# State-space impulse responses with full-width stationary operands, and a batch's outputs turned directly ahead of the next batch's readout

## The chip, the cores and the metric

One NeuronCore of one Trainium2 chip runs the whole program. Its engines work side by side, each through its own instructions strictly in order: TensorE (PE in the rows; its weight loads, PEld, are a track of their own and may run beside a matmul), VectorE (DVE), ScalarE (ACT), GpSimd (POOL) and SyncE (SP). The last two mostly issue transfers here. Engines wait for each other through semaphores that only count up. The metric is the device time of one launch in microseconds. The kernel before has a median of 3036.04 us over 3 runs (3035.94 to 3036.09).

## The reference

The program is one layer of a state-space and pooling block followed by an attention and feed-forward block, 512 tokens wide 2048, all in fp32. What matters here is the state-space mixer, 64 groups of 16 channels with 64 complex states:

```python
bu_re = jnp.einsum('blgc,gnc->blgn', u32, bb_re)
bu_im = jnp.einsum('blgc,gnc->blgn', u32, bb_im)
...
_, _, s_re, s_im = lax.associative_scan(
    _scan_combine, (a_re_t, a_im_t, bu_re, bu_im), axis=1)
y = (jnp.einsum('blgn,gcn->blgc', s_re, c_re.astype(f32))
     - jnp.einsum('blgn,gcn->blgc', s_im, c_im.astype(f32))
     + d_skip.astype(f32).reshape(N_SSM_GROUPS, SSM_GROUP) * u32)
```

The mixer's input is a quarter of `rmsnorm(x) @ w_in`, a product of 512 x 2048 with 2048 x 4096.

## The kernel before, in words

The input product is cut into 32 units n = 0 to 31 of 128 output columns. A unit is 16 tiles with three matmuls each (`products`, lines L1539 to L1541): the weights are split into a high and a low part (WH by ScalarE, WL by VectorE), the activations too (XH, XL), and high x high, high x low and low x high are added up in a PSUM bank. Between two units TensorE's program has small blocks of the state-space mixer. The 64 groups are treated in eight batches t of eight groups, and the 512 tokens in 64 chunks of 8 (CQ = 8, NCH = 64). For a batch:

- VectorE forms H, the output rows times powers of the transition (`impulse`), and BF, the input rows (`drive_rows`). TensorE multiplies them in `kernels` (L1673): for each group g the 16 columns of BF are the stationary operand, 128 columns of H move, and 16 rows come out in banks 2 and 3. ScalarE copies these rows to KS (`kernel_copies`, which counts ks_ready), and SyncE lays them out eight times as the banded matrix TZ (`kernel_rows`).
- VectorE forms G, TensorE turns it (`drives_turned`, L1684, banks 4 and 5), ScalarE copies it to GT.
- `chunk_states` (L1696): GT x U, the states that each chunk adds, in bank 6. ScalarE copies them to SL; SyncE swaps the two halves of the partitions into SSW (`states_swapped`); VectorE runs the scan over chunks (`scan`, L2306), which gives RR.
- SyncE swaps RR into RSW (`scan_swapped`); VectorE forms SV, the state carried into each chunk (`carried`, L2316 and L2319, counts sv_ready).
- `readout` (L1714), bank 7: first 8 matmuls U x TZ (within a chunk), then 8 matmuls SV x H (carried in). Each has a stationary operand of 64 columns, and they alternate between the upper and the lower 64 output rows.
- ScalarE copies bank 7 to YS (`token_copy`, counts ys_ready). `tokens_turned` (L1724) turns YS into bank 2 by 16 matmuls of 64 x 64 with the identity, again in alternating halves, and counts yt_done. VectorE adds the result to the input times d_skip (`y_out`, L2324, counts y_read).

Nothing schedules this at run time; the order is written out by the unit number n. On TensorE, behind unit 8 + 3t stand `chunk_states(t)` and `kernels(t + 1)`, behind unit 9 + 3t `readout(t)`, behind unit 10 + 3t `drives_turned(t + 1)` and `tokens_turned(t)`; batch 7 is shifted by one unit. The other engines have loops over the same n. A plain fp32 matmul is one instruction in the program and two records in the trace (a transpose is one record), so that `kernels` has 8 matmuls and 16 records for a batch.

The YS buffer lies at the same place as RSW (60 K). SyncE's copy into RSW has these waits, which the diff does not touch:

```python
def scan_swapped(t):

    sp.wait_ge(r_ready, t + 1)
    if t >= 1:
        sp.wait_ge(yt_done, t)
    sp.dma_start(RSW[0:64, :], RR[64:128, :]).then_inc(r_swapped, 16)
    sp.dma_start(RSW[64:128, :], RR[0:64, :]).then_inc(r_swapped, 16)
```

In SyncE's loop it stands in turn n = 9 + 3t, behind `states_swapped(t)` and the load of RAW for unit n + 3 (for t = 7 in turn 29).

Of the kernel before, what the change touches and what calls it, by code (L numbers as in the profile page):

```python
# [25 lines left out]
P = 128  # L26
S = 512
# [5 lines left out]
SSM_GROUPS, SSM_C, SSM_N = 64, 16, 64  # L33
MIX_TILES = 8
# [94 lines left out]
CQ = 8  # L129
# [42 lines left out]
def build(nc, w_units, w_ada, c_row, x_t, p_t, vec_d, con_d, mask_d, ssm_par, ssm_bc, w_pool_d,  # L172
# [3 lines left out]
    def at(name, off, shape, dt=FP32):  # L176
        return nc.alloc_sbuf_tensor_at(name, shape, dt, offset=base + off)

    K = 1024
# [41 lines left out]
    IDENT = CON[:, C_ID:C_ID + P]  # L221
# [18 lines left out]
    SSW = at("SSW", 56 * K, [P, S])  # L240
    RR = at("RR", 58 * K, [P, S])
    RSW = at("RSW", 60 * K, [P, S])
    YS = at("YS", 60 * K, [P, S])
    MAG = at("MAG", 62 * K, [P, BG, NCH])
    FR = at("FR", 64 * K, [P, BG, NCH])
    SP = at("SP", 54 * K, [P, 20, SSM_GROUPS])
# [4 lines left out]
    S0 = B0 + 16 * K  # L251
# [10 lines left out]
    BC = at("BC", S0 + 40480, [P, 4, BG * SSM_C])  # L262
    BF = at("BF", S0 + 42528, [P, 2, BG * SSM_C])
    FK = at("FK", S0 + 43552, [P, BG, NCH])

    ROPE = at("ROPE", 48 * K, [P, 4, S])
    MASK = at("MASK", 56 * K, [P, 3, S])
# [102 lines left out]
    with ExitStack() as ctx:  # L370
        PS = ctx.enter_context(nc.psum_tensor("PS", [P, 8, S], FP32))
# [5 lines left out]
        def sem(name):  # L377
            return ctx.enter_context(nc.semaphore(name))
# [21 lines left out]
        h_ready, k_done, ks_ready, tz_loaded, g_ready, g_turned, gt_ready = (  # L400
            sem(n) for n in ("h_ready", "k_done", "ks_ready", "tz_loaded", "g_ready", "g_turned", "gt_ready"))
        s_done, s_copied, s_swapped, s_used, r_ready, r_swapped, sv_ready = (
            sem(n) for n in ("s_done", "s_copied", "s_swapped", "s_used", "r_ready", "r_swapped", "sv_ready"))
        y_done, ys_ready, yt_done, y_read = (sem(n) for n in ("y_done", "ys_ready", "yt_done", "y_read"))
# [573 lines left out]
        def _(act):  # L978
# [29 lines left out]
            def whole_turns(t):  # L1008

                act.wait_ge(f_ready, t + 1)  # L1010
                act.activation(FK[:, :, :], FR[:, :, :], ACT.Identity, bias=CON[:, C_MAGIC:C_MAGIC + 1])
                act.drain()
# [44 lines left out]
            def token_copy(t):  # L1057
                if t >= 1:

                    act.wait_ge(yt_done, t)  # L1060
                act.wait_ge(y_done, t + 1)
                act.activation(YS[:, :].rearrange("p (j g c) -> p g j c", j=CQ, g=4),
                               PS[:, 7, :].rearrange("p (g j c) -> p g j c", j=CQ, g=4), ACT.Copy)\
                   .then_inc(ys_ready, 1)

# [36 lines left out]
            for n in range(4, N_IN):  # L1102
                t = scan_batch(n)
# [344 lines left out]
            for t in range(FULL_K):  # L1448
                ins = act.activation(TA[:, 1, t, 0:HALF_S], RES[:, t, HALF_S:S], ACT.Identity, bias=DS[:, t:t + 1])
# [3 lines left out]
            for t in range(FULL_K):  # L1453
                b = 3 * DT + FULL_K + t
                ins = act.activation(TC[:, t, 0:HALF_S], RES[:, FULL_K + t, HALF_S:S], ACT.Identity,
                                     bias=MOD[:, b:b + 1])
# [73 lines left out]
        def _(pe):  # L1530
# [133 lines left out]
            def kernels(t):  # L1664

                pe.wait_ge(h_ready, t + 1)
                if t >= 1:
                    pe.wait_ge(ks_ready, t)
                if t >= 2:
                    pe.wait_ge(y_read, t - 1)  # L1670
                for g in range(BG):
                    c = SSM_C * g
                    ins = pe.matmul(PS[0:16, 2 + g // 4, g % 4 * P:(g % 4 + 1) * P], BF[:, 0, c:c + SSM_C],  # L1673
                                    H[:, t % 2, g, 0:P], start=True, stop=True)
                    if g % 4 == 3:
                        ins.then_inc(k_done, 1)
# [23 lines left out]
            def readout(t):  # L1700
                s = t % 2

                pe.wait_ge(tz_loaded, 16 * CQ * (t + 1))
                if t >= 1:
                    pe.wait_ge(ys_ready, t)
                for first in (True, False):
                    if not first:
                        pe.wait_ge(sv_ready, t + 1)
                    for q in range(4):
                        for par in range(2):  # L1710
                            g = 4 * par + q
                            w, x = (U[:, s, g, :], TZ[:, g, :]) if first else (
                                SV[:, g, 0:NCH], H[:, s, g, SSM_C:SSM_C + P])
                            ins = pe.matmul(PS[64 * par:64 * par + 64, 7, q * P:(q + 1) * P], w, x,  # L1714
                                            start=first and q == 0, stop=not first, skip_group_check=True)
                ins.then_inc(y_done, 1)

            def tokens_turned(t):

                pe.wait_ge(ys_ready, t + 1)  # L1720
                pe.wait_ge(ks_ready, min(t + 2, MIX_TILES))
                for j in range(CQ):
                    for par in range(2):
                        ins = pe.matmul(PS[64 * par:64 * par + 64, 2, NCH * j:NCH * j + NCH],  # L1724
                                        YS[:, 64 * j:64 * j + 64], IDENT[:, 64 * par:64 * par + 64],
                                        start=True, stop=True, skip_group_check=True)
                ins.then_inc(yt_done, 1)

# [9 lines left out]
            for n in range(2, N_IN):  # L1738
                input_unit(n)
                if n == 2:  # L1740
                    ones_sum()
                if 8 <= n <= 26 and n % 3 == 2:
                    chunk_states((n - 8) // 3)
                    kernels((n - 5) // 3)
                if n == 6:
                    kernels(0)
                if 9 <= n <= 27 and n % 3 == 0:
                    readout((n - 9) // 3)
                if 7 <= n <= 25 and n % 3 == 1:
                    drives_turned((n - 7) // 3)  # L1750
                if n == 27:
                    drives_turned(7)
                if n == 28:
                    chunk_states(7)
                if 10 <= n <= 28 and n % 3 == 1:
                    tokens_turned((n - 10) // 3)
                if n == 29:
                    readout(7)
                if n == 30:
                    tokens_turned(7)  # L1760

            halves = [[(8 * h + k, k) for k in range(8)] for h in range(2)]
            for j in range(8):
                s, n = j % 2, U_GLU + j
# [300 lines left out]
        def _(v):  # L2065
# [255 lines left out]
            def y_out(t):  # L2321

                v.wait_ge(yt_done, t + 1)
                v.scalar_tensor_tensor(out=PROJ[:, t, :], in0=PROJ[:, t, :], scalar=VEC[:, V_DS + t:V_DS + t + 1],  # L2324
                                       in1=PS[:, 2, :], op0=ALU.mult, op1=ALU.add).then_inc(y_read, 1)
# [45 lines left out]
            for n in range(2, N_IN):  # L2371
                if 8 <= n <= 26 and n % 3 == 2:
                    angles((n - 8) // 3)
                if n == 28:
                    angles(7)
                if 11 <= n <= 29 and n % 3 == 2:
                    y_out((n - 11) // 3)
                if n == 31:
                    y_out(7)
                if n == 27:  # L2380
                    drives(7)
                if n >= 3:
                    prep_lo(n + 1, (n + 1) % 2)
                if n == 3:
                    exponents()
                if n == 4:
                    drive_factors()
                if n == 5:
                    transition_powers()
                    drive_rows(0)  # L2390
                if 5 <= n <= 26 and n % 3 == 2:
                    impulse((n - 5) // 3)
                if 8 <= n <= 26 and n % 3 == 2:
                    fractions((n - 8) // 3)
                if n == 28:
                    fractions(7)
                if 7 <= n <= 25 and n % 3 == 1:
                    drives((n - 7) // 3)
                    drive_rows((n - 4) // 3)
                t = scan_batch(n)  # L2400
                if t is not None:
                    scan(t)
                    carried(t)
                if n == N_IN - 1:
                    for k in range(MIX_TILES):
                        v.wait_ge(xh_ready, X_GLU + k + 1)
                        v.tensor_tensor(GL[:, k, :], PROJ[:, k, :], f32(GH[:, k, :]), ALU.subtract)\
                         .then_inc(x_ready, 1)
                evac_in(n)
# [648 lines left out]
            a, b, lo, hi = (slice(0, FULL_K), slice(FULL_K, DT), slice(0, HALF_S), slice(HALF_S, S))  # L3058
# [14 lines left out]
            for t in range(FULL_K):  # L3073
                ins = v.scalar_tensor_tensor(out=TA[:, 1, t, hi], in0=RES[:, t, hi], scalar=DS[:, t:t + 1],
                                             in1=f32(TA[:, 1, t, lo]), op0=ALU.add, op1=ALU.subtract)
# [10 lines left out]
            for t in range(FULL_K):  # L3086
                m = 3 * DT + FULL_K + t
                ins = v.scalar_tensor_tensor(out=TC[:, t, hi], in0=RES[:, FULL_K + t, hi], scalar=MOD[:, m:m + 1],
                                             in1=f32(TC[:, t, lo]), op0=ALU.add, op1=ALU.subtract)
# [109 lines left out]
            c = PLAIN_CHUNKS - 1  # L3199
# [136 lines left out]
```

## Time and profile before

| | us |
|---|---|
| median of 3 runs | 3036.04 |
| the profiled execution, span | 3035.4 |
| TensorE busy | 3011.8 (99%) |
| VectorE busy | 2268.8 (75%) |
| ScalarE busy | 1243.8 (41%) |
| GpSimd busy | 362.1 (12%) |
| chain that ended last, TensorE's share | 98% |
| windows of the input units, 91 to 432 us: TensorE busy | 341.00 |

Only the span of the profiled execution is shown for it, no device time of its own. A row of a timeline is one instruction or a run of equal ones: its start from the span's start, its length to the end of the last, engine, line and operation, output <- inputs, shape, count, and in brackets how long the engine was idle before and who ended that. Matmuls are pipelined: the length of one holds its way through the array, so prices are read from start to start. A window row has the length of the stretch and for each engine the busy time and the count; PEclk is the granted TensorE clock, 1.00 for the level of 2.4 GHz and 0.50 for 1.2 GHz. The program's names of tiles are given without buffer numbers.

### The profile page before, as it was taken

To read this page: it belongs to the slowest core of one execution; us is meant where nothing else is said; L and a number is where in the kernel's file an instruction comes from. 1 tells how busy PE (TensorE), PEld (TensorE's weight loads), DVE (VectorE), ACT (ScalarE), POOL (GpSimd) and SP (SyncE) were. 2 spreads that over 40 slices of the span, in tenths; PEclk is the share of its full clock that TensorE was granted. 3 is DMA by queue.
4 is the path that set the end of the run, shared out by engine and by line. 5 is a ranking of instruction groups with operands and counts; after the bars stand their busy time and mean duration, and the time that the engine had idled before them with its cause. 6 is when DMAs were issued, how large, how long until landed. Compare 5 with 4: busy or idle time off the path is not lost.

```text
span 3035.4 us, 41372 instructions
## 1 busy us (share of the span) xinstructions
PE 3011.8 (99%) x15348; PEld 2530.7 (83%) x15348; DVE 2268.8 (75%) x2837; ACT 1243.8 (41%) x1593; POOL 362.1 (12%) x524
## 2 busy tenths in 40 slices
PE   8999999999999999999999999999999999999998
PEld 7888887888888888888888788888888888888887
DVE  6766646868887666777765788888888888888875
ACT  5223352213234333444442454444444444344433
POOL 0211100111110111001000200000000000011123
PEclk9999999999999999999999999999999999999999
DMA  5444353876765444344342256666666666588774
GB/s 189 140 133 136 123 205 118 325 274 219 269 232 198 167 166 166 123 162 165 126 153 97 111 177 180 176 176 179 174 172 171 169 175 180 184 228 228 228 227 160
DMA packets 120797, 544.95 MB, mean 180 GB/s; under 512 B 22304, under 2 KB 22576, under 8 KB 80880
## 3 DMA queue, kind: packets, MB, share of 16 engines
q1 hardware_dynamic: 63856, 321.15, 29.9%
q0 software_dynamic: 53232, 195.38, 23.3%
q10 hardware_dynamic: 3600, 26.98, 2.3%
q8 instruction: 67, 1.10, 0.1%
q14 instruction: 42, 0.34, 0.0%
HBM read 434.13 MB, written 37.76 MB: 155 GB/s over the span
## 4 chain that ended last, share of the span: by engine, by line
PE 98%; DVE 2%; DMA 0%; ACT 0%; issue 0%; DVEq 0%; ACTq 0%
PE PS L1983 18%; PE PS L1539 16%; PE PS L1541 15%; PE PS L1540 15%; PE PS L1986 9%; PE PS L2053 3%; PE PS L2052 3%; PE PS L2050 3%; PE PS L2018 1%; PE PS L2019 1%; PE PS L2020 1%; PE PS L1852 1%; PE PS L1592 1%; PE PS L1594 1%; PE PS L1593 1%; PE PS L1840 1%
## 5 line engine op out<-in xcount | busy, mean ns | idle before, releaser
L1539 PE MATMUL PS<-XHL,WH 128*128 128x512 f32 x1952 | 765.5, 392 | 0.3 <-DVE BB L2550 0.2
L1541 PE MATMUL PS<-XHL,WL 128*128 128x512 f32 x1952 | 760.0, 389 | 0.0
L1540 PE MATMUL PS<-XHL,WH 128*128 128x512 f32 x1952 | 759.6, 389 | 0.0
L982 ACT ACTIVATE WH<-RAW 128x2048 fp32r<-128x2048 f32 x137 | 262.0, 1913 | 475.1 <-PE PS L1541 472.4
L1539 PEld LDWEIGHTS PS<-XHL,WH 128*128 128x128 f32 x1952 | 366.4, 188 | 82.6 <-issue 5.7
L1541 PEld LDWEIGHTS PS<-XHL,WL 128*128 128x128 f32 x1952 | 366.4, 188 | 76.9
L1540 PEld LDWEIGHTS PS<-XHL,WH 128*128 128x128 f32 x1952 | 366.5, 188 | 75.0 <-issue 0.2
L2069 DVE TENSOR_TENSOR WL<-RAW,WH 128x2048 fp32r<-128x2048 f32 x136 | 311.0, 2287 | 86.4 <-ACT WH L982 86.3
L1327 ACT ACTIVATE QH<-RAW 128x1024 fp32r<-128x1024 f32 x210 | 222.1, 1059 | 250.0 <-PE PS L1986 237.2
L1983 PE MATMUL PS<-XHL,QH 128*128 128x512 f32 x1008 | 316.5, 395 | 0.0
L2923 DVE TENSOR_TENSOR QL<-RAW,QH 128x1024 fp32r<-128x1024 f32 x210 | 256.4, 1222 | 59.4 <-ACT QH L1327 59.4
L1986 PEld LDWEIGHTS PS<-XHL,QL 128*128 128x128 f32 x1008 | 189.4, 188 | 44.8
L1983 PE MATMUL PS<-TA,QH 128*128 128x512 f32 x672 | 211.0, 395 | 0.0
L1986 PE MATMUL PS<-XHL,QL 128*128 128x256 f32 x1008 | 198.0, 278 | 0.0
L2923 DVE TENSOR_TENSOR QL<-SUM,QH 128x1024 fp32r<-128x1024 f32 x84 | 102.9, 1225 | 75.9 <-ACT QH L1327 75.9
L1983 PEld LDWEIGHTS PS<-XHL,QH 128*128 128x128 f32 x1008 | 153.5, 189 | 0.1
L1986 PEld LDWEIGHTS PS<-TA,QL 128*128 128x128 f32 x672 | 126.2, 188 | 29.8
L2109 DVE CUSTOM_DVE_ANT_0 ADA<-ADA,CB 128x1024 f32<-128x1024 f32 x112 | 130.7, 1219 | 2.0 <-DMA ADA<-w_ada_dram 2.0
L1986 PE MATMUL PS<-TA,QL 128*128 128x256 f32 x672 | 132.0, 278 | 0.0
L698 POOL DMA_DIRECT2D ADAQ<-w_ada_dram x80 | 51.0, 637 | 561.9 <-DVE MODH L2109 266.0
L2050 PE MATMUL PS<-WH,FOPH 128*128 128x512 f32 x296 | 115.1, 389 | 0.0
L2052 PE MATMUL PS<-WL,FOPH 128*128 128x512 f32 x296 | 115.1, 389 | 0.0
(442 smaller groups left out, 5271.3 us busy)
## 6 DMA issues: line engine op xcount, KB each, us to landing
RAW<-w_units_dram SPq DMA_DIRECT2D x228, 1024.0 KB, 4.9
ADA<-w_ada_dram POOLq DMA_DIRECT2D x112, 512.0 KB, 5.6
ADAQ<-w_ada_dram POOLq DMA_DIRECT2D x80, 512.0 KB, 5.5
A<-w_units_dram SPq DMA_DIRECT2D x32, 1024.0 KB, 8.0
SUM<-RAW POOLq DMA_DIRECT2D x42, 512.0 KB, 4.6
RAW<-SUM POOLq DMA_DIRECT2D x42, 512.0 KB, 4.5
FRAW<-f_dram SPq DMA_DIRECT2D x4, 2048.0 KB, 13.0
A<-A POOLq DMA_DIRECT2D x8, 1024.0 KB, 7.5
```

What stands on the lines that cost most here:

```text
L982: act.activation(WH[:, slot, :], RAW[:, slot, :], ACT.Copy).then_inc(hi_ready, 1)
L1327: act.activation(QH[:, slot, :], weight(s2, j), ACT.Copy).then_inc(q_hi, 1)
L1539: pe.matmul(PS[:, bank, :], wh, rh[:, x, :], start=k == 0, stop=False)
L1540: pe.matmul(PS[:, bank, :], wh, rl[:, x, :], start=False, stop=False)
L1541: ins = pe.matmul(PS[:, bank, :], wl, rh[:, x, :], start=False, stop=k == n - 1)
L1983: pe.matmul(in_halves(PS[:, bank, :]), QH[:, slot, k * P:(k + 1) * P], fast_data(j, k), start=k == 0 and j not in (3, 5, 6), stop=False, s ...
L1986: ins = pe.matmul(PS[:, bank, 0:HALF_S], QL[:, slot, k * P:(k + 1) * P], fast_data(j, k)[:, HIGH.get(j, 0), :], start=False, stop=k == FUL ...
L2050: pe.matmul(out, fh, wh[:, k * S:(k + 1) * S], start=first and k == 0, stop=False, skip_group_check=True)
L2052: pe.matmul(out, fh, wl[:, k * S:(k + 1) * S], start=False, stop=False, skip_group_check=True)
L2069: v.tensor_tensor(WL[:, slot, :], RAW[:, slot, :], f32(WH[:, slot, :]), ALU.subtract)\
L2109: v.tensor_tensor_reduce(w, w, c, 1.0, 0.0, ALU.mult, ALU.add, (MODH if half else MOD)[:, t:t + 1]).then_inc(ada_used, 1)
L2923: v.tensor_tensor(QL[:, slot, :], weight(s2, j), f32(QH[:, slot, :]), ALU.subtract).then_inc(q_lo, 1)
```

## The change

Three things are edited.

1. `kernels`: the stationary operand is 128 columns of BF, from the group's first column on, in place of the group's 16; the output takes all 128 rows. Only the first 16 rows are copied to KS, as before.
2. `tokens_turned(t)` stands behind unit 12 + 3t, ahead of `readout(t + 1)`, for t = 0 to 5; `tokens_turned(6)` stands behind unit 29, ahead of `readout(7)`; `tokens_turned(7)` stays behind unit 30. VectorE's `y_out(t)` moves from the head of turn 11 + 3t to that of turn 14 + 3t (6: turn 30). The semaphore values follow: the tokens wait for one more batch of ks_ready and for y_read of the batch before, the impulse responses for y_read of one batch less.
3. YS has a place of its own for batches 0 to 6; batch 7 keeps the place shared with RSW (YS7).

```diff
--- before.py
+++ after.py
@@ -240,7 +240,7 @@
     SSW = at("SSW", 56 * K, [P, S])
     RR = at("RR", 58 * K, [P, S])
     RSW = at("RSW", 60 * K, [P, S])
-    YS = at("YS", 60 * K, [P, S])
+    YS7 = at("YS7", 60 * K, [P, S])
     MAG = at("MAG", 62 * K, [P, BG, NCH])
     FR = at("FR", 64 * K, [P, BG, NCH])
     SP = at("SP", 54 * K, [P, 20, SSM_GROUPS])
@@ -262,6 +262,7 @@
     BC = at("BC", S0 + 40480, [P, 4, BG * SSM_C])
     BF = at("BF", S0 + 42528, [P, 2, BG * SSM_C])
     FK = at("FK", S0 + 43552, [P, BG, NCH])
+    YS = [at("YS", S0 + 45600, [P, S])] * (MIX_TILES - 1) + [YS7]
 
     ROPE = at("ROPE", 48 * K, [P, 4, S])
     MASK = at("MASK", 56 * K, [P, 3, S])
@@ -1059,7 +1060,7 @@
 
                     act.wait_ge(yt_done, t)
                 act.wait_ge(y_done, t + 1)
-                act.activation(YS[:, :].rearrange("p (j g c) -> p g j c", j=CQ, g=4),
+                act.activation(YS[t][:, :].rearrange("p (j g c) -> p g j c", j=CQ, g=4),
                                PS[:, 7, :].rearrange("p (g j c) -> p g j c", j=CQ, g=4), ACT.Copy)\
                    .then_inc(ys_ready, 1)
 
@@ -1666,11 +1667,12 @@
                 pe.wait_ge(h_ready, t + 1)
                 if t >= 1:
                     pe.wait_ge(ks_ready, t)
-                if t >= 2:
-                    pe.wait_ge(y_read, t - 1)
+                if t >= 3:
+                    pe.wait_ge(y_read, t - 2)
+                drive_rows = BF[:, :, :].rearrange("p a n -> p (a n)")
                 for g in range(BG):
                     c = SSM_C * g
-                    ins = pe.matmul(PS[0:16, 2 + g // 4, g % 4 * P:(g % 4 + 1) * P], BF[:, 0, c:c + SSM_C],
+                    ins = pe.matmul(PS[:, 2 + g // 4, g % 4 * P:(g % 4 + 1) * P], drive_rows[:, c:c + P],
                                     H[:, t % 2, g, 0:P], start=True, stop=True)
                     if g % 4 == 3:
                         ins.then_inc(k_done, 1)
@@ -1718,11 +1720,13 @@
             def tokens_turned(t):
 
                 pe.wait_ge(ys_ready, t + 1)
-                pe.wait_ge(ks_ready, min(t + 2, MIX_TILES))
+                pe.wait_ge(ks_ready, min(t + 3, MIX_TILES))
+                if t >= 1:
+                    pe.wait_ge(y_read, t)
                 for j in range(CQ):
                     for par in range(2):
                         ins = pe.matmul(PS[64 * par:64 * par + 64, 2, NCH * j:NCH * j + NCH],
-                                        YS[:, 64 * j:64 * j + 64], IDENT[:, 64 * par:64 * par + 64],
+                                        YS[t][:, 64 * j:64 * j + 64], IDENT[:, 64 * par:64 * par + 64],
                                         start=True, stop=True, skip_group_check=True)
                 ins.then_inc(yt_done, 1)
 
@@ -1744,6 +1748,8 @@
                     kernels((n - 5) // 3)
                 if n == 6:
                     kernels(0)
+                if 12 <= n <= 27 and n % 3 == 0:
+                    tokens_turned((n - 12) // 3)
                 if 9 <= n <= 27 and n % 3 == 0:
                     readout((n - 9) // 3)
                 if 7 <= n <= 25 and n % 3 == 1:
@@ -1752,9 +1758,8 @@
                     drives_turned(7)
                 if n == 28:
                     chunk_states(7)
-                if 10 <= n <= 28 and n % 3 == 1:
-                    tokens_turned((n - 10) // 3)
                 if n == 29:
+                    tokens_turned(6)
                     readout(7)
                 if n == 30:
                     tokens_turned(7)
@@ -2373,8 +2378,10 @@
                     angles((n - 8) // 3)
                 if n == 28:
                     angles(7)
-                if 11 <= n <= 29 and n % 3 == 2:
-                    y_out((n - 11) // 3)
+                if 14 <= n <= 29 and n % 3 == 2:
+                    y_out((n - 14) // 3)
+                if n == 30:
+                    y_out(6)
                 if n == 31:
                     y_out(7)
                 if n == 27:
```

TensorE's program behind unit 10, before; CON,G are the drives turned, CON,YS the tokens turned:

```order
L1540 MATMUL PS<-XHL,WH 128x512
L1541 MATMUL PS<-XHL,WL 128x512
L1684 MATMUL PS<-CON,G 128x128 x8
L1724 MATMUL PS<-CON,YS 64x64 x16
L1539 MATMUL PS<-XHL,WH 128x512
```

and of the change:

```order
L1541 MATMUL PS<-XHL,WH 128x512
L1542 MATMUL PS<-XHL,WL 128x512
L1686 MATMUL PS<-CON,G 128x128 x8
L1540 MATMUL PS<-XHL,WH 128x512
L1541 MATMUL PS<-XHL,WH 128x512
```

The tokens no longer stand behind the drives; the next unit follows at once.

TensorE behind unit 11, before; U,GT are the chunk states, H,BF the impulse responses:

```order
L1541 MATMUL PS<-XHL,WL 128x512
L1696 MATMUL PS<-U,GT 128x64 x8
L1673 MATMUL PS<-H,BF 16x128 x8
L1539 MATMUL PS<-XHL,WH 128x512
L1540 MATMUL PS<-XHL,WH 128x512
```

and of the change:

```order
L1542 MATMUL PS<-XHL,WL 128x512
L1698 MATMUL PS<-U,GT 128x64 x8
L1675 MATMUL PS<-H,BF 128x128 x8
L1540 MATMUL PS<-XHL,WH 128x512
L1541 MATMUL PS<-XHL,WH 128x512
```

The block stays where it was; the stationary operand is 128 wide in place of 16.

TensorE behind unit 12, before; TZ,U and H,SV are the two halves of the readout:

```order
L1541 MATMUL PS<-XHL,WL 128x512
L1714 MATMUL PS<-TZ,U 64x128 x8
L1714 MATMUL PS<-H,SV 64x128 x8
L1539 MATMUL PS<-XHL,WH 128x512
L1540 MATMUL PS<-XHL,WH 128x512
```

and of the change:

```order
L1542 MATMUL PS<-XHL,WL 128x512
L1728 MATMUL PS<-CON,YS 64x64 x16
L1716 MATMUL PS<-TZ,U 64x128 x8
L1716 MATMUL PS<-H,SV 64x128 x8
L1540 MATMUL PS<-XHL,WH 128x512
L1541 MATMUL PS<-XHL,WH 128x512
```

The tokens of the batch before now stand directly ahead of the readout.

## Rows read from the trace of the kernel before

**Rows 1.** the page, its first line
```profile
span 3035.4 us, 41372 instructions
```

**Rows 2.** windows: length, busy us (instructions) by engine, PEclk, DMA share, GB/s
```profile
91.00:432.00 341.00, 341.00 (x2051) 283.00 (x2051) 208.34 (x227) 114.30 (x134) 49.95 (x92) 1.00 0.44 138
```

**Rows 3.** TensorE's waits: who waited for whom, total us, times, longest
```profile
PE PS L1592 <- DVE XHL L2907: 3.5, 4, 1.7
```

**Rows 4.** timeline of TensorE, readout: start us, length us, instruction, operands, count
```profile
253.26 0.39 PE L1539 MATMUL PS<-XHL,WH 128*128 128x512 f32 x1
...
253.71 0.39 PE L1541 MATMUL PS<-XHL,WL 128*128 128x512 f32 x1
254.03 1.09 PE L1714 MATMUL PS<-TZ,U 128*64 128x128 f32 x16
254.96 1.04 PE L1714 MATMUL PS<-H,SV 128*64 128x128 f32 x16
...
256.27 0.40 PE L1540 MATMUL PS<-XHL,WH 128*128 128x512 f32 x1
```

**Rows 5.** timeline of TensorE, drives turned alone
```profile
104.90 0.40 PE L1541 MATMUL PS<-XHL,WL 128*128 128x512 f32 x1
105.14 1.03 PE L1684 MATMUL PS<-CON,G 128*128 128x128 f32 x8
...
106.25 0.40 PE L1540 MATMUL PS<-XHL,WH 128*128 128x512 f32 x1
```

**Rows 6.** timeline of TensorE, the first batch's impulse responses, alone
```profile
91.95 0.39 PE L1541 MATMUL PS<-XHL,WL 128*128 128x512 f32 x1
92.27 1.92 PE L1673 MATMUL PS<-H,BF 128*16 128x128 f32 x16
...
94.45 0.40 PE L1540 MATMUL PS<-XHL,WH 128*128 128x512 f32 x1
```

**Rows 7.** timeline of TensorE, drives and tokens turned
```profile
225.93 0.39 PE L1541 MATMUL PS<-XHL,WL 128*128 128x512 f32 x1
...
227.13 1.15 PE L1724 MATMUL PS<-CON,YS 128*64 128x64 f32 x32
...
228.55 0.40 PE L1540 MATMUL PS<-XHL,WH 128*128 128x512 f32 x1
```

**Rows 8.** timeline of TensorE, the attention's value products and what follows
```profile
980.16 2.39 PE L1852 MATMUL PS<-VS,PT 128*128 128x128 f32 x20
982.39 0.60 PE L1832 MATMUL PS<-CON,VT 128*128 128x128 f32 x4
```

**Rows 9.** timeline of the weight loads, first batch; in brackets idle before
```profile
92.27 1.64 PEld L1673 LDWEIGHTS PS<-H,BF 128*16 128x16 f32 x16 [0.35 <-issue]
```

**Rows 10.** line L1852, weight loads: ns min/median/max
```profile
L1852 PEld LDWEIGHTS PS<-VS,PT x320: 187/192/192, 979.9 to 1537.7; 128*128 128x128 f32 x160
```

**Rows 11.** line L1673, weight loads: ns min/median/max
```profile
L1673 PEld LDWEIGHTS PS<-H,BF x128: 92/97/97, 92.3 to 365.0; 128*16 128x16 f32 x128
```

**Rows 12.** timeline of VectorE, one batch; in brackets idle before and releaser
```profile
228.33 0.75 DVE L2324 SCALAR_TENSOR_TENSOR PROJ<-PROJ,VEC,PS 128x512 f32<-128x512 f32 x1 [0.68 <-PE PS L1724]
...
248.20 1.23 DVE L2306 TENSOR_TENSOR_SCAN RR<-MAG,TMP 128x512 f32<-128x512 f32 x1
...
252.29 0.69 DVE L2316 TENSOR_TENSOR RSW<-RSW,SIN 128x512 f32<-128x512 f32 x1 [2.08 <-DMA RSW<-RR]
253.06 0.69 DVE L2319 TENSOR_TENSOR SV<-TMP,RSW 128x512 f32<-128x512 f32 x1
```

**Rows 13.** timeline of SyncE's issues, same batch
```profile
249.46 0.46 SPq L497 DMA_DIRECT2D RSW<-RR  x1
```

**Rows 14.** windows around two pauses of TensorE, columns as in rows 2
```profile
1722.20:1725.70 3.50, 1.56 (x6) 0.68 (x5) 3.50 (x6) 2.34 (x5) 3.50 (x4) 1.00 0.00 0
1725.70:1729.10 3.40, 3.40 (x8) 2.68 (x9) 3.40 (x5) 2.17 (x5) 3.21 (x4) 0.50 0.09 36
...
908.60:912.00 3.40, 1.94 (x7) 1.35 (x8) 3.27 (x6) 1.98 (x4) 0.00 (x0) 1.00 1.09 453
```

## The prediction, made blind

> **What bounds the kernel now.** I read five views, in this order. The page gives the span, 3035.4 us [rows 1]; the median of the runs shown is 3036.0 us, so 0.6 us lies outside the span. I make the sum on the span and add the 0.6 at the end. The table of windows says that from 91 to 432 us (the input projections with the state-space work between them, the only stretch that the change touches) TensorE is busy for 341.00 us of 341.00, at a granted clock of 1.00 [rows 2]. The list of TensorE's waits has nothing there; the longest behind the start of the program is 1.7 us, much later [rows 3]. So time is gained here only in TensorE's own instructions, and every new wait of TensorE is paid in full. TensorE's timeline then gives the price of each small block between two projection units, and the timelines of VectorE and SyncE give the chain that feeds the second half of the readout.
>
> The price of a block is read between starts: from the last projection matmul ahead of it (L1541) to the second one behind it (L1540), less the 0.45 us that two matmuls take in the dense stream (253.26 to 253.71) [rows 4].
> - readout (L1714, twice 16 records): 256.27 - 253.71 - 0.45 = 2.11 us [rows 4]
> - drives turned (L1684, 8 records, operand of 128 columns): 106.25 - 104.90 - 0.45 = 0.90 us [rows 5]
> - impulse responses (L1673, 16 records, operand of 16 columns): 94.45 - 91.95 - 0.45 = 2.05 us [rows 6]
> - drives and tokens turned: 228.55 - 225.93 - 0.45 = 2.17 us, so 1.27 us for the tokens (L1724, 32 records of 64 columns) [rows 7]
>
> **The change part by part.** (a) Full width. The impulse responses keep their 8 x 16 = 128 records, but each loads 128 columns and not 16; the 112 further output rows are not read. The full-width drives cost 0.90/8 = 0.11 us a record with their edges [rows 5]. The nearest row to the new form, the attention's value products (128 columns, 128 moving), takes (982.39 - 980.16)/20 = 0.11 us too [rows 8]. At that, a batch costs 16 x 0.1125 = 1.80 us, not 2.05: 0.25 us less. I read the 0.25 as the edges of a narrow block: it starts 0.32 us after the last L1541 where a full-width one starts after 0.24, and its weight loads sat idle for 0.35 us and began only with its own matmuls [rows 4 to 6, 9]. Eight batches: 2.0 us gained. Bounds: a load lasts 192 ns in place of 97 [rows 10, 11]; all of it bare is 128 x 0.095 = 12.2 us lost; on the other side 0.35 us a batch, 2.8 us, if the whole idle time is an edge. I take 2.0, since both full-width rows say it.
>
> The Trainium skill, "TensorE: Matmul & The Clock Gate", Part 3, speaks against this edit: a weight load overlaps running matmuls only when it goes to another row group. By it these full-height loads would lie bare, and part (a) would lose the 12 us. The trace disagrees: the value products use all rows too, and a load of 192 ns fits in 0.11 us a record [rows 8, 10]. It stays as a rival.
>
> (b) Tokens ahead of the readout. For t = 0 to 6 the tokens of batch t are turned directly ahead of readout t + 1: seven moves; batch 7 stays alone. Both blocks have operands of 64 columns in alternating halves, so one pair of narrow edges goes each time: 7 x 0.25 = 1.8 us gained. Tokens in the new place cost 1.27 - 0.25 = 1.0 us. That two such blocks join without an edge shows inside the readout, whose second 16 records follow 0.93 us after the first [rows 4]. Bounds: 0 (the edge comes back between them) and 0.35 x 7 = 2.5 us.
>
> (c) A wait that was free and now decides. The readout's second half needs the carried states SV. These need the two swapped halves RSW, which SyncE copies in `scan_swapped(t)`. That function waits for yt_done at t, "tokens of t - 1 are turned", since the output buffer used to share its place with RSW. The output buffer has moved away, but this wait stands. Until now those tokens ended two units earlier; now they end just ahead of the same readout. The order around it: tokens of t - 1, then (behind them only) the RSW copy, VectorE's product and SV, then the second half of readout t. TensorE, strictly in order, stands at that second half, and everything behind it too. Counted from the last L1541 ahead, X:
> - tokens start at X + 0.32 as narrow blocks do, their records last 1.15 us [rows 4, 7], and another engine sees their end 0.05 us later (227.13 + 1.15 = 228.28, VectorE's y_out at 228.33) [rows 7, 12]: X + 1.52
> - the copy: today VectorE's scan ends at 248.20 + 1.23 = 249.43, SyncE issues at 249.46, and VectorE takes RSW up at 252.29 [rows 12, 13]: 2.86 us, two transfers one after the other. X + 4.38
> - from there to the end of SV: 253.06 + 0.69 - 252.29 = 1.46 us [rows 12]. X + 5.84, and some 0.07 us until TensorE starts: X + 5.9
>
> Without that chain the second half would start at X + 0.32 + 1.0 + 0.93 = X + 2.25. The wait is 3.65 us. It falls on readouts 1 to 7 (t = 0 waits for nothing): 7 x 3.65 = 25.6 us lost. Today the same chain starts at the scan's end and is over at 253.75, before its records at 254.96 [rows 4, 12]; that cover of 1.2 us is gone with the order. Bounds: with no other traffic the copies may be quicker, but they are issued one behind the other and no row shows them under 2.8 us, so 3.3 us a wait at least (23 us); with a weight load in the way, perhaps 4.2 us (29 us).
>
> Nothing else queues up from it, I think: VectorE's evacuation, its WL and the RAW load that SyncE issues next lie as far from the next unit's start as before, since that start is late by the same amount. The other new waits of TensorE (KS of t + 2 copied; y_read of the batch before) are for work that ends a whole unit of 48 matmuls earlier, and I put them at nothing. The activation over batches 0 to 6 waits for y_out of 6 and then for the copy of readout 7, which comes later; nothing.
>
> (d) The clock. TensorE will stand still for over 3 us seven times. This trace shows once what such a thing does: from 1722.20 to 1725.70 us TensorE was busy for 1.56 us of 3.50, after its wait of 1.7 us, and the next 3.40 us ran at a granted clock of 0.50, the level of 1.2 GHz, with 8 records where the dense stream has 15 [rows 3, 14]: 7 x 0.227 = 1.6 us lost. A milder pause, 1.94 us busy of 3.40, had no such effect [rows 14]. My waits are longer than either, so I count a fall each time, and 1.45 us on the mean, since part of a low stretch may lie over the wait itself: 7 x 1.45 = 10 us. Bounds: 0, and 2 x 1.6 x 7 = 22 us if each fall lasts twice as long.
>
> Sum: -2.0 - 1.8 + 25.6 + 10 = +31.8 us. 3035.4 + 31.8 + 0.6 = 3067.8 us, 1.05% above 3036.0. Behind 432 us TensorE is again as good as always busy, so nothing gives this back. What can be told from no change is about 0.2%, 6.1 us.
>
> **The rivals.**
> 1. The waits come, the clock stays up: 3035.4 - 3.8 + 25.6 + 0.6 = 3057.8 us. For it: small blocks stand close to the waits, and the milder pause did nothing. Against it: the row at 0.50 followed a pause half as long. Chance 0.15.
> 2. The clock stays down about twice as long per wait: 3057.8 + 22 = 3080 us. For it: the stretch behind a fall begins with the small records of the readout. Against it: in the one fall seen, the dense matmuls ran at full speed again after 3.4 us. Chance 0.05.
> 3. The other side: the wait for yt_done is over when SyncE comes to it, or the carried states are not needed so soon, so the edges alone count: 3036.0 - 3.8 = 3032.2 us. It would take tokens that end before VectorE's scan, more than 4 us ahead of the unit's end; TensorE issues them behind the unit. It decides for "not slower" only where the wait per readout is under 0.5 us. Chance 0.03.
> 4. Bare weight loads in (a) on top: 3067.8 + 2.0 + 12.2 = 3082 us. It begins to count where more than a few ns of the 95 lie bare. Chance 0.03.
>
> **How the numbers follow.** The forecast, waits and falls of the clock, has 0.74; its own range is 3061 to 3073 us (23 to 29 us of waits, 6 to 13 us of clock). The range takes in rival 1: 3056.5 to 3073.5 us. Slower by over 0.2%: 0.96. Within 0.2%: 0.03, faster: 0.01, both from rival 3.
>
> **What would show it.** The list of waits has TensorE's readout records (H, SV) waiting for VectorE's SV seven times, about 3.5 us each, and VectorE's product with RSW waiting longer for its transfer than now. SyncE's RSW copies start 1.5 us behind the end of a unit. Without readout and waits: impulse responses alone near 1.80 us, drives alone 0.90 us in every batch. The granted clock is 0.50 in stretches just behind the waits, with matmuls 0.43 us apart. I am wrong on (c) if readout records start less than 5 us after X; on (d) if the clock stays at 1.00 through the stretch; on (a) if impulse records lie more than 0.12 us apart. If (c) comes as told and the span is under 3050 us, the waits were made good by something I have overlooked.

## The result and the profile after

| | before | changed |
|---|---|---|
| median, us (4 runs each) | 3036.00 | 3073.61 |
| lowest to highest | 3035.94 to 3036.09 | 3072.61 to 3073.87 |
| ratio | | 1.0122, 95% interval 1.011 to 1.0134 |
| span of the profiled execution | 3035.4 | 3072.1 |

The change costs 37.6 us where 31.8 were forecast. The time lies 5.8 us above the forecast and 0.1 us above the upper end of its range.

Again the page and the windows come first: the stretch of the input units, now 91 to 470 us, and in it two stretches around a readout (columns as in rows 2).

```profile
span 3072.1 us, 41372 instructions
```

```profile
91.00:470.00 379.00, 353.07 (x2054) 295.95 (x2053) 208.38 (x227) 115.06 (x134) 49.89 (x92) 0.95 0.40 126
174.30:181.10 6.80, 5.72 (x25) 4.62 (x26) 6.56 (x7) 0.60 (x1) 1.09 (x2) 0.50 0.48 143
222.10:225.50 3.40, 3.40 (x20) 2.79 (x21) 3.31 (x3) 0.60 (x1) 1.09 (x2) 0.50 0.37 98
```

The stretch ends later than before (470 us and not 432) because all of the loss lies in it. Where TensorE was busy for every microsecond [rows 2], it now stands still for 379.00 - 353.07 = 25.9 us, and the mean granted clock is 0.95, with stretches at 0.50. The list of TensorE's waits names who is waited for (total us, times, longest):

```profile
PE PS L1716 <- DVE SV L2324: 25.9, 7, 4.5
```

Line L1716 is the readout, L2324 the end of `carried`. The list has exactly the seven entries of step (c). One readout in the timeline of TensorE; X of the prediction is the row at 216.10:

```profile
216.10 0.39 PE L1542 MATMUL PS<-XHL,WL 128*128 128x512 f32 x1
216.42 1.15 PE L1728 MATMUL PS<-CON,YS 128*64 128x64 f32 x32
217.40 1.05 PE L1716 MATMUL PS<-TZ,U 128*64 128x128 f32 x16
222.01 1.96 PE L1716 MATMUL PS<-H,SV 128*64 128x128 f32 x16 [3.57 <-DVE SV L2324]
223.90 0.80 PE L1540 MATMUL PS<-XHL,WH 128*128 128x512 f32 x1
224.49 0.63 PE L1541 MATMUL PS<-XHL,WH 128*128 128x512 f32 x1
224.92 0.63 PE L1542 MATMUL PS<-XHL,WL 128*128 128x512 f32 x1
```

The issues of SyncE and the timeline of VectorE around it:

```profile
217.66 0.46 SPq L498 DMA_DIRECT2D RSW<-RR  x1
218.16 0.60 SPq L499 DMA_DIRECT2D RSW<-RR  x1
```

```profile
220.50 0.69 DVE L2321 TENSOR_TENSOR RSW<-RSW,SIN 128x512 f32<-128x512 f32 x1 [7.68 <-DMA RSW<-RR]
221.26 0.69 DVE L2324 TENSOR_TENSOR SV<-TMP,RSW 128x512 f32<-128x512 f32 x1
```

The reader can follow the chain: tokens end at 216.42 + 1.15 = 217.57, SyncE issues 0.09 us later, VectorE takes RSW up 2.84 us behind that, SV is finished at 221.95, TensorE goes on at 222.01. That is X + 5.91; the prediction had X + 5.9. VectorE sat idle for 7.68 us where it was 2.08 us [rows 12]. Behind the wait the second half of the readout takes 1.96 us in place of 1.04 [rows 4], and the projection matmuls lie 0.43 us apart: the clock.

The first batch's impulse responses and drives, alone, in the timeline of TensorE; they answer to [rows 5, 6]:

```profile
91.31 0.40 PE L1542 MATMUL PS<-XHL,WL 128*128 128x512 f32 x1
91.54 1.95 PE L1675 MATMUL PS<-H,BF 128*128 128x128 f32 x16
...
93.56 0.39 PE L1541 MATMUL PS<-XHL,WH 128*128 128x512 f32 x1
```

```profile
103.99 0.39 PE L1542 MATMUL PS<-XHL,WL 128*128 128x512 f32 x1
104.22 1.03 PE L1686 MATMUL PS<-CON,G 128*128 128x128 f32 x8
...
105.33 0.40 PE L1541 MATMUL PS<-XHL,WH 128*128 128x512 f32 x1
```

The impulse responses cost 93.56 - 91.31 - 0.45 = 1.80 us (forecast 1.80, before 2.05) and start 0.23 us behind L1542, no longer 0.32. The drives cost 105.33 - 103.99 - 0.45 = 0.89 us (before 0.90).

### The profile page after: what moved, and what is told of

Its sections match the earlier page's. It is cut to its first block, busy times and chain, and to the rows that moved or that the text cites. A ratio compares the mean times of both kernels' runs of the same rounds, so it can differ in the third digit from the quotient of the medians.

```text
span 3072.1 us, 41372 instructions
## 1 busy us (share of the span) xinstructions
PE 3021.1 (98%) x15348; PEld 2541.2 (83%) x15348; DVE 2268.0 (74%) x2837; ACT 1243.6 (40%) x1593; POOL 361.8 (12%) x524
## 4 chain that ended last, share of the span: by engine, by line
PE 97%; DVE 2%; DMA 1%; SPq 0%; ACT 0%; issue 0%; DVEq 0%; ACTq 0%
PE PS L1988 18%; PE PS L1540 15%; PE PS L1541 15%; PE PS L1542 15%; PE PS L1991 9%; PE PS L2055 3%; PE PS L2057 3%; PE PS L2058 3%; PE PS L2023 1%; PE PS L2025 1%; PE PS L2024 1%; PE PS L1857 1%; PE PS L1593 1%; PE PS L1595 1%; PE PS L1594 1%; PE PS L1845 1%
## 5 line engine op out<-in xcount | busy, mean ns | idle before, releaser
L1542 PE MATMUL PS<-XHL,WL 128*128 128x512 f32 x1952 | 762.5, 391 | 0.0
L1542 PEld LDWEIGHTS PS<-XHL,WL 128*128 128x128 f32 x1952 | 368.2, 189 | 77.4
```

The costliest lines, as they stand in the source:

```text
L1542: ins = pe.matmul(PS[:, bank, :], wl, rh[:, x, :], start=False, stop=k == n - 1)
```

## The experiments

Block prices below are read as in the prediction. The kernel before was run again beside the experiments, with medians of 3036.30 us in the first group and 3036.45 us in the second; times are compared through these. The edits of the wait, of the move and of the spare work are shown against the changed kernel, those of the operand's width against the kernel before.

**The wait taken away.**

```diff
             def scan_swapped(t):

                 sp.wait_ge(r_ready, t + 1)
-                if t >= 1:
-                    sp.wait_ge(yt_done, t)
```

> The changed kernel without SyncE's wait for yt_done ahead of the RSW copy; the output buffer of batches 0 to 6 has its own place, so the copy overwrites nothing that is still read. If the wait and the clock falls behind it are the whole loss (my theory): no TensorE wait at the readout's second half, granted clock 1.00 through the stretch, tokens with readout at 3.1 us by the block price, and about 3032 us (3031.4 to 3032.8), 0.13% under the kernel before. If the loss had another cause as well (late copies of KS, y_read, a dearer readout), it stays above 3040 us. If the merged blocks save nothing by themselves, 3034 us.

Measured: 3031.97 us, ratio 0.9986 (0.9977 to 0.9995). TensorE has no wait in the stretch. The timeline of the same readout:

```profile
169.01 0.39 PE L1540 MATMUL PS<-XHL,WL 128*128 128x512 f32 x1
169.33 1.15 PE L1726 MATMUL PS<-CON,YS 128*64 128x64 f32 x32
170.31 1.05 PE L1714 MATMUL PS<-TZ,U 128*64 128x128 f32 x16
171.19 1.04 PE L1714 MATMUL PS<-H,SV 128*64 128x128 f32 x16
172.16 0.50 PE L1538 MATMUL PS<-XHL,WH 128*128 128x512 f32 x1
172.50 0.40 PE L1539 MATMUL PS<-XHL,WH 128*128 128x512 f32 x1
```

The second half starts at X + 2.18, and tokens with readout cost 172.50 - 169.01 - 0.45 = 3.04 us. One stale wait was the whole loss: without it the kernel is 41.6 us faster than the changed one and 4.3 us faster than the kernel before. This is the version that beats both.

**Full width alone**, put into the kernel before.

```diff
-                    ins = pe.matmul(PS[0:16, 2 + g // 4, ...], BF[:, 0, c:c + SSM_C],
+                    ins = pe.matmul(PS[:, 2 + g // 4, ...], drive_rows[:, c:c + P],
```

> The kernel before with the full-width stationary operand of the impulse responses alone. Edges of narrow blocks are what is saved: block price of the first batch 1.80 us and of states with impulse responses about 3.56 us, 3034.1 us in all (1.9 us less than before). Rival of bare weight loads: up to 3048 us, records of the impulse responses 0.2 us apart. Rival that a 16-column operand costs no edge: 3036 us, no change.

Measured: 3034.47 us, 1.8 us less than before; the ratio 0.9994 (0.9985 to 1.0003) does not exclude no change, so the block price decides. It is the one of the changed kernel, 93.88 - 91.62 - 0.45 = 1.81 us for the first batch. In the other seven batches the block stands behind the chunk states; the two together fell from 120.92 - 116.68 - 0.45 = 3.79 us to 120.11 - 116.08 - 0.45 = 3.58 us, and 0.25 + 7 x 0.21 = 1.7 us is close to the 1.8 us of the time. Bare weight loads are excluded: the 16 records follow each other at (93.56 - 91.86)/16 = 0.11 us, with loads of 192 ns.

**The move alone**, that is the changed kernel without SyncE's wait (as in the first experiment) and with the 16-column operand:

```diff
-                drive_rows = BF[:, :, :].rearrange("p a n -> p (a n)")
...
-                    ins = pe.matmul(PS[:, 2 + g // 4, ...], drive_rows[:, c:c + P],
+                    ins = pe.matmul(PS[0:16, 2 + g // 4, ...], BF[:, 0, c:c + SSM_C],
```

> The changed kernel without SyncE's wait and with the old 16-column operand, so the move of the tokens alone. If two narrow blocks side by side share one pair of edges: tokens with readout 3.1 us, drives alone 0.9 us, 3034.0 us in all (seven moves, 0.25 to 0.33 us each, 1.8 to 2.3 us less than before). If the edge comes back between tokens and readout: 3036 us and 3.35 us for the joint block.

Measured: 3033.84 us, 2.5 us less than before, ratio 0.9992 (0.9983 to 1.0001). By the block price the joint block costs 3.04 us, as above. Before: 2.17 + 2.11 = 4.28 us; now 0.89 + 3.04 = 3.93 us: 0.35 us a move, 7 x 0.35 = 2.5 us. The two parts add up: 1.8 + 2.5 = 4.3 us.

**Spare work in the wait**: eight matmuls between the two halves of readouts 1 to 7.

```diff
+                        if t >= 1:
+                            pe.wait_ge(s_copied, t + 1)
+                            for _ in range(8):
+                                pe.matmul(PS[:, 6, 0:2 * P], IDENT, CON[:, C_ID:C_ID + 2 * P], start=True, stop=True,
+                                          skip_group_check=True)
                         pe.wait_ge(sv_ready, t + 1)
```

> The changed kernel with eight spare matmuls of 256 columns (identity times constants, 16 records, about 3.45 us) between the two halves of readouts 1 to 7, where TensorE stands still; they write into bank 6, which is free there, and nothing reads them. If a good 11 us of the loss are the clock (theory): the wait shrinks to 0.1 to 0.3 us for each readout, the second half still starts 5.9 us after the last projection matmul, the clock stays at 1.00, and the time is 3057.8 us (3057 to 3060). If the clock falls whatever TensorE does in the wait, or costs nothing: 3073 us. If the waits were not set by the RSW copy, the second half starts later by what the spare matmuls take.

Measured: 3062.44 us (1.0085, 1.0069 to 1.01). The clock stayed at 1.00 through the stretch, as the theory has it, but the time is 4.6 us above the forecast one. In three of the readouts the second half starts at X + 5.93 to 5.95, in three at X + 6.5 and in one much later. That one in the timeline of TensorE:

```profile
256.95 0.39 PE L1542 MATMUL PS<-XHL,WL 128*128 128x512 f32 x1
257.27 1.15 PE L1733 MATMUL PS<-CON,YS 128*64 128x64 f32 x32
258.25 1.05 PE L1721 MATMUL PS<-TZ,U 128*64 128x128 f32 x16
259.23 3.72 PE L1713 MATMUL PS<-CON 128*128 128x256 f32 x16
264.69 1.09 PE L1721 MATMUL PS<-H,SV 128*64 128x128 f32 x16 [1.74 <-DVE SV L2329]
```

and its copies and VectorE:

```profile
258.52 0.46 SPq L498 DMA_DIRECT2D RSW<-RR  x1
```

```profile
263.18 0.69 DVE L2326 TENSOR_TENSOR RSW<-RSW,SIN 128x512 f32<-128x512 f32 x1 [9.50 <-DMA RSW<-RR]
```

Issue to use took 4.66 us and not 2.84. So here the copies, not the spare matmuls, were late. The trace also shows what goes with it. The view of the transfers from 258.5 to 263.2 us has one more queue than the same view around a copy of usual length (214.5 to 217.4 us), the one for instructions (packets, MB, share of 16 engines):

```profile
q8 instruction: 1, 0.02, 1.2%
```

The ten profiled kernels have 80 such pairs of copies. Five took 3.4 to 4.7 us, four of them in this kernel and one in the changed one (its last), and in each of the five this queue moved one packet meanwhile. The other 75 took 2.82 to 2.89 us, and in none of them did it. Whether that transfer itself holds the copies up was not tested.

**Half of the spare work**: `range(4)` in place of `range(8)`.

> As the kernel with eight spare matmuls, but four (8 records, about 1.75 us), so that TensorE stands still for some 1.8 us in each of the seven readouts. The waits are as long in all, the second half starts 5.9 us behind the last projection matmul. If a pause of 1.8 us is enough for the clock to fall (one row of the kernel before speaks for it, with 1.7 us): about 3070 us, falls in most of the seven. If it takes more: no fall, 3058 to 3062 us.

Measured: 3058.59 us (1.0073, 1.0056 to 1.009). The window over the stretch, and one readout:

```profile
91.00:454.00 363.00, 351.43 (x2106) 294.09 (x2105) 207.91 (x227) 114.96 (x134) 49.89 (x92) 1.00 0.41 131
```

```profile
169.17 0.39 PE L1542 MATMUL PS<-XHL,WL 128*128 128x512 f32 x1
169.49 1.15 PE L1733 MATMUL PS<-CON,YS 128*64 128x64 f32 x32
170.47 1.04 PE L1721 MATMUL PS<-TZ,U 128*64 128x128 f32 x16
171.44 1.99 PE L1713 MATMUL PS<-CON 128*128 128x256 f32 x8
175.08 1.09 PE L1721 MATMUL PS<-H,SV 128*64 128x128 f32 x16 [1.65 <-DVE SV L2329]
```

TensorE stands still seven times for about 1.65 us, and the clock never falls in the stretch. The second half starts at X + 5.91 as in the changed kernel; all seven are within 0.04 us here. So this kernel has the waits without the falls: 3058.59 - 3031.97 = 26.6 us for the waits (with the edges of the spare block in it), and 3073.61 - 3058.59 = 15.0 us for the clock.

**Three waits in place of seven.**

```diff
-                if t >= 1:
+                if 1 <= t <= 3:
                     sp.wait_ge(yt_done, t)
```

> The changed kernel with SyncE's wait for yt_done kept for batches 1 to 3 alone. If each wait pays for itself and nothing adds up or is given back: three sevenths of the loss against the kernel without it (3031.97 us), 3 x 5.95 = 17.9 us, so 3049.8 us, with three readouts that start 5.9 us behind the last projection matmul and four that start 2.2 us behind. If the waits were only the sign of a slower stream elsewhere, the time would not go by their number.

Measured: 3049.09 us (1.0042, 1.0026 to 1.0059), 17.1 us above the kernel without waits; 5.7 us for a wait. The list of waits:

```profile
PE PS L1716 <- DVE SV L2324: 10.7, 3, 3.6
```

The loss goes by the number of waits. Each of the three brought a fall of the clock.

**64 and 96 columns** as the stationary operand, in the kernel before (`BF` from c to c + 64, or c + 96).

> The kernel before with 64 columns as the stationary operand of the impulse responses (16 are used, 64 rows come out). If the edge belongs to any operand that fits half the array: block price of the first batch 2.05 us, start 0.32 us behind the projection matmul, weight loads idle ahead of it. If it belongs to the 16 columns only: 1.80 us and 0.23 us. No reading of the time: the block price decides.

> The kernel before with 96 columns as the stationary operand of the impulse responses. The Trainium skill (TensorEngine Tiling, Tiling Modes) names column tiles of 128, 64 and 32, and 96 fits the full one only: block price 1.80 us, start 0.23 us behind the projection matmul. If only exactly 128 columns are free of the edge: 2.05 us and 0.32 us.

The first batch with 64 columns, in the timelines of TensorE and of the weight loads (the latter was asked up to 93 us only, so that its row has 10 of the 16 loads):

```profile
91.72 0.39 PE L1541 MATMUL PS<-XHL,WL 128*128 128x512 f32 x1
92.04 1.96 PE L1674 MATMUL PS<-H,BF 128*64 128x128 f32 x16
...
94.27 0.40 PE L1540 MATMUL PS<-XHL,WH 128*128 128x512 f32 x1
```

```profile
92.04 1.06 PEld L1674 LDWEIGHTS PS<-H,BF 128*64 128x64 f32 x10 [0.35 <-issue]
```

and with 96:

```profile
91.54 0.40 PE L1541 MATMUL PS<-XHL,WL 128*128 128x512 f32 x1
91.77 1.91 PE L1674 MATMUL PS<-H,BF 128*96 128x128 f32 x16
...
93.75 0.40 PE L1540 MATMUL PS<-XHL,WH 128*128 128x512 f32 x1
```

With 64 columns the edge is there: a start 0.32 us behind the matmul ahead, loads idle for 0.35 us, block price 94.27 - 91.72 - 0.45 = 2.10 us. With 96 it is gone: start at 0.23 us, block price 93.75 - 91.54 - 0.45 = 1.76 us. One execution each gave 3037.35 and 3034.46 us beside 3036.45 us; by themselves these two would decide nothing.

## Why the prediction was right, point by point

| step | forecast, us | measured, us | from |
|---|---|---|---|
| (a) full width | -2.0 | -1.8 | its kernel alone |
| (b) move of the tokens | -1.8 | -2.5 | its kernel alone |
| (c) the wait for the RSW copy, seven times | +25.6 | about +26.6 | four spare matmuls against no wait |
| (d) falls of the clock | +10 | about +15.0 | changed kernel against four spare matmuls |
| sum | +31.8 | +37.6 | |

The four measured terms are differences between kernels and add up to 37.3 us, the distance from the kernel before as it ran beside the experiments (3036.30 us). Waits and clock were forecast as to their kind, place and number; the sizes of (b), (c) and (d) were too small, that of (d) by the most.

(a) The mechanism held and the size was 0.2 us high: the 0.25 us of the first batch was taken for all eight, and behind the chunk states it is 0.21. The edges of a narrow block were its cost, and a load of 192 ns lies hidden at the pitch that the value products have [rows 8, 10]. The rule of the Trainium skill that was weighed ("TensorE: Matmul & The Clock Gate", Part 3: weight loads overlap only across row groups) does not hold here: the records with full-height loads of 192 ns lie 0.11 us apart. What does fit is the page TensorEngine Tiling (Array Packing) of the Trainium skill: its Tiling Modes list column tiles of 128, 64 and 32, and its Key Properties say that a change of mode drains the engine. The runs with 64 and 96 columns agree with that, edge and no edge. They show where the border lies, not that a drain is what happens at it.

(b) The size was low because I took 0.25 us for a pair of edges, from the impulse responses, where two widths differ as well. The four block prices separate the two: 2.05 us with 16 columns [rows 6], 2.10 with 64, 1.76 with 96, 1.80 with 128. The step from 64 to 96, where the edges go, is 0.34 us; the wider operand costs about 0.04 us on either side of it. A pair of edges that goes without a change of width is worth 0.35 us, which stood as the bound, and equals the idle time of the weight loads in [rows 9].

(c) The mechanism and its times were right to 0.1 us: the second half at X + 5.91 and not at X + 2.18, so 3.73 us a wait where 3.65 were forecast. The last readout is the exception: its copies took 3.77 us from issue to use, the fifth of the late pairs, and TensorE waited 4.5 us. The kernel with four spare matmuls has no late pair, so that in the table this 0.9 us is part of the difference that stands for (d), not of (c). The edges of the spare blocks, about 0.06 us each, go the other way. No queue behind the wait added anything, and KS, y_read and the activation at the end cost nothing, as the run without the wait shows.

(d) Here the forecast was mis-sized: 7 x 1.45 us against 7 x 2.1. The clock fell at each of the seven waits, but three of the low stretches lasted 6.8 us and four 3.4 us; the 6.8 us were reckoned only as rival 2 and for all seven. A long one began while TensorE still stood (174.3 us, with the second half of that readout at 175.38), a short one near the end of the wait (222.07 us against 222.01). In the short one above, TensorE issued 20 records: the readout's second half of 16, slow as well, and four projection matmuls. The price of each kind can be read at the twentieth projection matmul behind the block: in the changed kernel for a long stretch (X at 169.47) and a short one (X at 216.10), and in the kernel without the wait (X at 169.01).

```profile
183.51 0.39 PE L1541 MATMUL PS<-XHL,WH 128*128 128x512 f32 x1
229.07 0.39 PE L1541 MATMUL PS<-XHL,WH 128*128 128x512 f32 x1
176.60 0.39 PE L1539 MATMUL PS<-XHL,WH 128*128 128x512 f32 x1
```

They stand at X + 14.04, X + 12.97 and X + 7.59. Less the 3.73 us of the wait, the long stretch costs 2.72 us and the short one 1.65 us, and all seven read this way lie within 0.03 us of these two prices. Three long and four short make 14.8 us. So the 1.6 us of the forecast was the right price of a short stretch. What failed in the term was the discount to 1.45, which took off a part of the low stretch for lying over the wait, and that none of the seven was taken for a long one: the stretches that began inside the wait, 1.1 us ahead of its end, were the long ones and cost more, not less.

Rival 1 (no fall) is what the kernel with four spare matmuls does, 3058.59 us against 3057.8 forecast for it. Rival 3 (edges alone) is the kernel without the wait, 3031.97 us against 3032.2. Rival 4 fell with the full-width kernel. Not settled: what decides between a short and a long stretch, and why single RSW copies land 0.6 to 1.8 us late when the instruction queue moves a packet.

Two numbers of the prediction don't hold, and neither moved the forecast. The 0.6 us "outside the span" compares a median with a profiled execution that had no time of its own; where one execution has both, the difference is 3073.8 - 3072.1 = 1.7 us. The forecast is in effect the median before plus 31.8 us. And the terms given beside its range, 29 us of waits and 13 us of clock on 3032.2 us, end at 3074.2 us, not at 3073.

## What to carry to other kernels

When work is moved, follow every semaphore that it counts to every engine that waits for it, also where the diff has no line: here SyncE's wait guarded a buffer that the change itself had moved away, and it turned 4.3 us of gain into 37.6 us of loss. On an engine that is always busy a wait of 3.6 us costs its own length and then the clock (5.95 us in all); where such a wait can't be removed, a few spare matmuls in it gave 15 us back. Small blocks with an operand of 16 or 64 columns cost about 0.35 us of edges in this full-width stream: widen them (to 128 columns saved 0.21 to 0.25 us a block here) or set two side by side (0.35 us).

## What was not expected of the hardware

- The clock's fall depends on more than the length of a pause. Every kernel has the same pause of 1.65 us in the feed-forward part and one of about 1.25 us behind it; a fall lay between them in the kernel before [rows 14] and in the one with three waits, and in none of the other eight. The kernel without the wait, with a window around both pauses:

```profile
1718.94 0.47 PE L1591 MATMUL PS<-XHL,WH 128*128 128x512 f32 x1 [1.65 <-DVE XHL L2912]
1730.68 0.50 PE L1591 MATMUL PS<-XHL,WH 128*128 128x512 f32 x1 [1.28 <-DVE XHL L2912]
```

```profile
1700.00:1740.00 40.00, 35.11 (x182) 28.58 (x181) 34.19 (x49) 19.77 (x35) 19.99 (x16) 1.00 0.34 131
```

  Seven pauses of 1.65 us (four spare matmuls) brought none, ten of 3.5 us and more (changed kernel, three waits) brought ten.
- A fall costs only where TensorE sets the pace. The same two pauses in the kernel before, with its fall between them:

```profile
1724.48 0.47 PE L1592 MATMUL PS<-XHL,WH 128*128 128x512 f32 x1 [1.66 <-DVE XHL L2907]
1736.21 0.50 PE L1592 MATMUL PS<-XHL,WH 128*128 128x512 f32 x1 [1.26 <-DVE XHL L2907]
```

  From one to the other it is 11.73 us, and 11.74 us without the fall: shorter waits for VectorE in between took up the slower matmuls. So the 1.6 us that the prediction calls lost at this fall was not lost there; the short stretches of the mixer, where TensorE waits for nobody behind them, did cost 1.65 us. The span of one profiled execution (3035.4 against 3029.9 us) shows 5.5 us between the kernel before and the one without the wait, where the medians show 4.3 us; of this 1.1 us is there ahead of the first block that differs (X at 91.95 and at 90.84 us).
- Once fallen, the clock was low for 3.4 us or for 6.8 us, nothing between.
- 96 columns cost slightly less than 128: 1.76 against 1.80 us for a block of 16 records.
